# Spreading the filler projections evenly over the attention slots of a decoder layer

## The reference

```python
z = u @ w_in
(fq, fk, fv, f_logit, gq, gk, gv, a_lr, g_r, gate_fox, gate_gla) = jnp.split(z, IN_OFFSETS, axis=-1)
o_fox = forgetting_attention(fq, fk, fv, log_f)      # 8 heads of 64, causal, query blocks of 128
o_gla = gla_chunked(gq, gk, gv, log_a)               # 4 heads, keys 64, values 128, chunks of 64
o_gla = rmsnorm(o_gla, gla_norm_g) * jax.nn.silu(g_r)
y = jax.nn.sigmoid(gate_fox) * (o_fox @ w_branch_fox) + jax.nn.sigmoid(gate_gla) * (o_gla @ w_branch_gla)
return y @ w_out
```

## Time and profile before

| | |
|---|---|
| median of 3 runs | 1118.76 us (1118.45 to 1118.97) |
| the profiled execution | 1118.97 us |
| span of the profile | 1117.2 us |
| TensorE busy | 1096.3 us, 98% of the span |
| VectorE busy | 576.8 us, 52% |
| ScalarE busy | 455.4 us, 41% |
| GpSimd busy | 55.3 us, 5% |
| DMA | 118.81 MB, 106 GB/s on average |

### The profile page before, as it was taken

The page is one execution under the profiler, slowest core; times in us unless marked ns, Lnnn a source line. Parts: engine busy times, 40 slices in busy tenths (PEclk is TensorE's granted clock), DMA queues, the critical chain, the costliest instruction groups (busy, mean ns, idle before and its releaser), DMA issues.

```text
span 1117.2 us, 14939 instructions
## 1 busy us (share of the span) xinstructions
PE 1096.3 (98%) x5910; PEld 944.4 (85%) x5910; DVE 576.8 (52%) x703; ACT 455.4 (41%) x661; POOL 55.3 (5%) x83
## 2 busy tenths in 40 slices
PE   7999999999999999998999999999999999999998
PEld 5888888888888888887878888889899999998886
DVE  5434443443333754456565333446788778763334
ACT  6222222232223474666765222325454454442222
POOL 2000000000000200000000000004600000000001
PEclk9999999999999999999999999999999999999999
DMA  9532333323322345222114335224423424233311
GB/s 299 152 104 85 112 94 94 94 94 104 102 95 60 106 141 151 76 76 58 38 39 127 98 96 169 94 76 161 160 76 99 129 76 140 87 132 133 98 52 76
DMA packets 133331, 118.81 MB, mean 106 GB/s; under 512 B 6416, under 2 KB 119072, under 8 KB 133280
## 3 DMA queue, kind: packets, MB, share of 16 engines
q1 hardware_dynamic: 131104, 113.38, 33.1%
q10 hardware_dynamic: 1456, 2.10, 0.9%
q0 software_dynamic: 720, 2.62, 0.6%
HBM read 109.70 MB, written 6.29 MB: 104 GB/s over the span
## 4 chain that ended last, share of the span: by engine, by line
PE 88%; DVE 5%; ACT 4%; issue 2%; DMA 1%; POOL 0%; SPq 0%; ACTq 0%; DVEq 0%; POOLq 0%
PE bank L1405 24%; PE bank L1395 12%; PE bank L1396 12%; PE bank L1397 12%; PE bank L1525 5%; PE bank L1524 5%; PE bank L1523 5%; PE bank L1637 1%; PE bank L1638 1%; PE bank L1639 1%; DVE w_lo L917 1%; PE bank L1460 1%; PE bank L1461 1%; PE bank L1462 1%; DMA raw<-in_ffn_w_up 1%
## 5 line engine op out<-in xcount | busy, mean ns | idle before, releaser
L917 DVE TENSOR_TENSOR w_lo<-raw,w_hi 128x1024 fp32r<-128x1024 f32 x130 | 166.1, 1279 | 213.2 <-ACT w_hi L503 213.1
L1395 PE MATMUL bank<-u_hi,w_hi 128*128 128x512 f32 x600 | 236.2, 394 | 0.2 <-issue 0.2
L1397 PE MATMUL bank<-u_hi,w_lo 128*128 128x512 f32 x600 | 233.8, 390 | 0.0
L1396 PE MATMUL bank<-u_lo,w_hi 128*128 128x512 f32 x600 | 233.7, 390 | 0.0
L503 ACT ACTIVATE w_hi<-raw 128x1024 fp32r<-128x1024 f32 x130 | 137.1, 1055 | 186.5 <-PE bank L1405 86.1
L1397 PEld LDWEIGHTS bank<-u_hi,w_lo 128*128 128x128 f32 x600 | 112.7, 188 | 24.0
L1395 PEld LDWEIGHTS bank<-u_hi,w_hi 128*128 128x128 f32 x600 | 112.8, 188 | 23.1 <-issue 0.5
L1396 PEld LDWEIGHTS bank<-u_lo,w_hi 128*128 128x128 f32 x600 | 112.9, 188 | 22.4 <-issue 0.2
L1405 PE MATMUL bank<-w_hi,a_hi 128*128 128x512 f32 x408 | 126.0, 390 | 0.0
L1405 PE MATMUL bank<-w_lo,a_hi 128*128 128x512 f32 x408 | 125.7, 389 | 0.0
L1405 PE MATMUL bank<-w_hi,a_lo 128*128 128x512 f32 x408 | 125.7, 389 | 0.0
(11 more groups left out here) (240 smaller groups left out, 1674.2 us busy)
## 6 DMA issues: line engine op xcount, KB each, us to landing
raw<-in_ffn_w_down SPq DMA_DIRECT2D x40, 512.0 KB, 3.4
raw<-in_w_in SPq DMA_DIRECT2D x40, 512.0 KB, 3.8
raw<-in_ffn_w_up SPq DMA_DIRECT2D x26, 512.0 KB, 3.9
raw<-in_ffn_w_gate SPq DMA_DIRECT2D x25, 512.0 KB, 3.8
raw<-in_ffn_w_gate SPq DMA_DIRECT2D x5, 1024.0 KB, 5.3
raw<-in_ffn_w_up SPq DMA_DIRECT2D x5, 1024.0 KB, 8.1
h_store<-h SPq DMA_DIRECT2D x2, 2048.0 KB, 9.9
h<-h_store SPq DMA_DIRECT2D x2, 2048.0 KB, 9.5
```

The costliest lines, as they stand in the source:

```text
L917: V.tensor_tensor(w_lo[:, slot(u), :], raw[:, slot(u), :], w_hi[:, slot(u), :].bitcast(F32), ALU.subtract).then_inc(lo_ready, 1)
L1395: mm(dst, w_hi[:, slot(u), w], rhs_hi[:, k - k0, :], start=k == k0, stop=False)
L1396: mm(dst, w_hi[:, slot(u), w], rhs_lo[:, k - k0, :], start=False, stop=False)
L1397: last = mm(dst, w_lo[:, slot(u), w], rhs_hi[:, k - k0, :], start=False, stop=k == k1)
```

## The change

From slot 16 on, the filler blocks are handed out two in each slot, where they were handed out 3, 3, 2 and none. The total of 40 blocks in slots 16 to 35 is the same.

```diff
         FILL, FILLED = {}, {}
         block_no = 0
         for sl in range(NS + 4):
-            for _ in range(4 if sl < 16 else (3, 3, 2, 0)[sl % 4]):
+            for _ in range(4 if sl < 16 else 2):
                 f, k = block_no // KD, block_no % KD
                 FILL.setdefault(sl, {}).setdefault(f, []).append(k)
                 if k == KD - 1:
                     FILLED[sl] = f
                 block_no += 1
```

## The result

The changed kernel takes 1130.69 us (median of 5 runs, 1129.24 to 1133.49) against 1118.76 us: 1.1% longer, ratio 1.011 with a 95% interval of 1.0088 to 1.0132. Two further executions on record, the profiled one and one of 1127.53 us, leave the median where it is. The forecast was 1129.2 us. The profiled execution took 1130.75 us, 11.8 more than the profiled one of before.

What follows compares the result with a forecast made beforehand. TensorE, at work nearly all of the 1117.2 us span, was taken as the bound. New waits of 7.4 us plus 3.0 for the clock made 10.4: 1129.4 for the profiled execution, 1129.2 against the median; range 1125.0 to 1133.0.

Steps and rivals of the forecast that it cites:

- The bound: Whole kernel: TensorE works nearly all of the 1117.2 us span, so reordering the same matmuls can only move its waits.
- The cause: Attention stage: read-out now falls just before the next filler, behind a late exponential, so TensorE waits for the bank.
- Slots 16 and 17: One block less in each, slot 18 starts unchanged: 1.4 us of new waiting; slot 17's wait 3.2 instead of 2.5.
- The four waits: First filler matmul of slots 20, 24, 28 and 32 waits 2.6, 1.6, 2.4 and 2.5 us for the read-out.
- The sum of the waits: Gate stage starts at 593.6 instead of 586.2, 7.4 us later, before any cost of the clock.
- the last read-out hidden: Slot 35: the last read-out is hidden behind that slot's value product as before; nothing given for the end.
- The clock: Granted clock falls after the waits of slots 20 and 32, at least as long as 2.49: two falls, 3.0 us.
- The rival of three or four falls: Attention stage: the clock falls after three or all four waits, +12 to +14, 1131 to 1133 us; chance 0.18.
- The outcome to which I gave 0.48: Attention stage: two falls of the clock (or one), two counted as 3.0 us; chance 0.48.
- The total: Whole kernel: 10.4 us longer, 1129.4 for the profiled execution, 1129.2 against the median.
- The other side: Rival: bank free when TensorE asks, even blocks cover waits in slots 25, 27, 31, 32, 34: -1.7, 1117.2 us; chance 0.04.

Runs made afterwards that it cites:

- the kernel that is kept busy: The changed kernel plus 11, 6, 9 and 11 extra unread matmuls ahead of the read-out waits in slots 20, 24, 28 and 32: 1125.91 us, ratio 1.0071.
- the first experiment: The kernel before with blocks from slot 16 on handed out 3, 3, 1, 1 instead of 3, 3, 2, 0: 1132.36 us, ratio 1.0132.
- fourth: The changed kernel with a finished filler's read-out ahead of row maximum (VectorE) and exponential (ScalarE) from slot 16 on: 1122.81 us, ratio 1.0053.
- fifth: The changed kernel with TensorE's filler blocks behind the linear attention and transposes in slots 20, 24, 28 and 32: 1122.09 us, ratio 1.0032.
- sixth: The kernel before with blocks of slots 16 to 19 handed out 3, 5, 0, 0: 1117.55 us, ratio 0.9997.
- eighth experiment: The changed kernel with blocks 3, 5, 0, 0 in slots 16 to 19, and filler behind the transposes in slots 24, 28, 32: 1121.43 us, ratio 1.0022.
- slot 17 kept busy: The kernel before with ten unread 512-column matmuls in slot 17's 2.5 us wait: 1115.71 us, ratio 0.9985.
- all waits kept busy: The kernel before with ten unread matmuls in slot 17 and 4, 1, 2, 5 more in slots 15, 27, 31, 32: 1116.95 us, ratio 0.9992.

## Why the prediction was right, step by step

**The bound.** Right. The work of TensorE and of the other engines stayed as it was, and the time went into TensorE's waits and its clock in this stage; behind the stage nothing moved (531.0 us in both).

**The cause.** Right, and shown by two kernels that move the same number of blocks: with fillers that end in slots 19, 23, 27 and 31 the ratio is 1.013, with fillers that end in 18, 22, 26 and 30 it is 1.001. Putting the read-out ahead of the exponential shrank the four waits from 8.5 us in all to 1.8, so its place in the queues was most of what made it late.

**Slots 16 and 17.** Right. The wait of slot 17 was forecast at 3.2 and is 3.16; slot 16 waits 0.77 us for L813 where the trace of before showed no such wait.

**The four waits.** Forecast 2.6, 1.6, 2.4 and 2.5; measured 2.53, 1.35, 2.10 and 2.49. The chain built from single rows of the old trace, with the read-out and the split taken out of it, held within 0.3 us at each place. The dates are a harder test, and the kernel that is kept busy gives them without the falls of the clock. Counted from the stage's first matmul, the fillers of slots 20, 24, 28 and 32 and the gate stage were forecast at 85.2, 103.0, 120.5, 138.8 and 147.5 us; there they start at 85.3, 103.1, 120.6, 139.0 and 147.7. The links can be seen on ScalarE's timeline of the changed kernel: the exponential of slot 19, followed by the read-out and the normalisation.

```profile
526.43 0.69 ACT L789 ACTIVATE scr<-bank,neg_max 128x512 f32<-128x512 f32 x1 [3.46 <-DVE neg_max L1264]
...
527.11 1.19 ACT L725 ACTIVATE qk<-bank 64x512 fp32r<-64x512 f32 x2
...
528.32 0.61 ACT L813 ACTIVATE scr<-scr,rinv 128x384 f32<-128x384 f32 x1
```

With the 2.15 us by which this stage starts earlier, the exponential stands at 528.6 on the old clock face, exactly where the prediction put it.

**The sum of the waits.** Forecast 7.4 us later at the gate stage; with the clock held up it is 7.55. One small wait was missed, 0.47 us for L1278 ahead of the gate stage (0.17 before); I had called the last read-out hidden.

**The clock.** This is the term that was mis-sized: 3.0 us forecast, as two falls of 1.5. It measured 6.35 in the first profile (two new falls, one of 10 us) and 4.9 in each of the others (three falls of 1.6). No run shows the 1.5 us of a fall that the sum takes; where a fall's cost can be told apart, the runs show 1.6 us (6.35 - 4.7, and 4.9 / 3), for 3.4 us at 0.50. With 0.43 us for a matmul that takes 0.23 at full speed this is 3.4 x (1 - 0.23 / 0.43) = 1.6. So the price was near, and the way of counting the falls was wrong. I had let the length of the wait decide, from the two rows I had. The runs show that it does not: no fall behind 3.2 us in slot 20 of the first experiment, falls behind 1.7 and 0.5 us in others, and both outcomes behind 2.1 us in the same kernel. The rival of three or four falls, which I gave 0.18, is what the profiles show: three falls in two of them, and in the first two falls that were down as long as four. Its price, 12 to 14 us, is that of the stage in all three (13.9, 12.4 and 12.5), and the 10.4 us of the forecast is not. The outcome to which I gave 0.48, two falls of 1.5 us, did not happen in any of them; the first profile has the two falls that I named, but one of them lasts. Of the nine executions only the one of 1127.53 us has a mean clock (0.995) that fits two short falls beside slot 17's; this is an estimate from 1.7 us of lost full-speed time for each fall.

The falls stand behind waits of 0.5 to 3.4 us, and they vary between the three profiles of the changed kernel. The start varies too: TensorE reaches its full pace at 12.6 to 17.2 us in the four profiles that the last section compares.

**The total** came out 1.5 us above the forecast. For the profiled execution the terms add up: 1130.75 against 1129.4 forecast for it is 1.35, and that is 3.35 from the clock and 0.15 from the waits, less the 2.15 by which its start was quicker. So part of the closeness is luck: a quick start that has nothing to do with the change hid most of what the clock term lacked. By the stage alone the miss is 3.5 us.

**The other side** did not happen. What it relied on, that an even spread covers the old waits in slots 27, 31 and 32, did happen (no wait for L813 after slot 16), but the new waits are larger.

## What to carry to other kernels

A block of cover work that ends in a shared buffer has two dates: when it runs, and when its last piece is done and the buffer must be read. Keep the gap that the read-out needs before the next use of the buffer, and see on the reading engines what stands ahead of the read-out there, and what the read-out itself pushes back. Moving cover from one wait to another is worth little when both waits hang on the same chain of another engine: the fourth, fifth, sixth and eighth experiment mostly changed which wait was paid, and with it where the clock fell. When TensorE's wait cannot be covered with useful work, price the clock as well, and test a few unread matmuls in it.

## What the runs showed of the hardware

The granted clock falls to 0.50 of full speed behind waits of very different length, from 0.5 us (slot 31 with slot 17 kept busy) to 3.4 us (slot 28 of the first experiment), and it stayed up behind one of 3.2 us (slot 20 there); the length alone does not say whether it will fall. Every fall in the profiled stages lasted 3.4 us, but for one that lasted 10.2 us, three times that, and cost 4.7. Where the cost of a short one can be told apart it is 1.6 us. The same wait of the same kernel, 2.1 us in slot 28 of the changed one, is followed by a fall in two executions and not in the third. What else decides it these runs do not settle. The kernel before was profiled once; its mean clock, 0.997 to 0.999 over all executions, leaves room for one or two falls (an estimate: 1.7 us lost of 1117 is 0.0015).

The executions of the kernel before lie in two groups about 2 us apart, 1115.7 to 1117.0 and 1118.1 to 1119.9 us. Between the two profiled executions the first 25 us show such a difference. The granted-clock column reads 1.00 over these 25 us in both, but the spacing of the matmuls does not agree with it. In the kernel before, pairs of matmuls at 14 us are 0.85 us apart, and from 17 us on 0.46:

```profile
14.03 1.05 PE L1587 MATMUL bank<-u_hi,w_hi 128*128 128x512 f32 x2
14.88 1.05 PE L1593 MATMUL bank<-u_hi,w_lo 128*128 128x512 f32 x2
...
17.19 0.62 PE L1593 MATMUL bank<-u_hi,w_lo 128*128 128x512 f32 x2
17.65 0.63 PE L1596 MATMUL bank<-u_lo,w_hi 128*128 128x512 f32 x2
```

In the changed kernel they are 0.46 apart already at 14 us:

```profile
13.70 0.62 PE L1593 MATMUL bank<-u_hi,w_lo 128*128 128x512 f32 x2
14.16 0.62 PE L1596 MATMUL bank<-u_lo,w_hi 128*128 128x512 f32 x2
```

TensorE reached its full pace about 4 us earlier (from 12.8 instead of 17.2 us on), though its first matmul came 0.95 us later, and the first matmul of L1395 stands at 21.43 instead of 23.57 us. The whole of the profile behind it is 2.15 us earlier. The two further executions of the changed kernel show it without a change between them: full pace from 15.8 and 12.6 us on, the attention stage begun at 445.51 and 443.76, both stages 152.6 us, and 1130.85 against 1129.14 us in all. Their difference of 1.7 us is the start. The falls of the clock inside the kernel do not make the two groups: with all waits kept busy, the six upper times, 1116.95 to 1117.65 us, all have a mean clock of 1.00. In all thirteen profiled executions on record, which have the same program ahead of the attention stage, the stage's first matmul stands either at 443.4 to 443.9 us (seven of them) or at 445.3 to 446.4 (six). That the start makes the groups is as good as shown by this; what makes the start was not tried.
